# A decoder step on Trainium2: page rows made between GpSimd's stores, retention's first transposes one job later, the sample mix in five steps, and low halves of the output weights on GpSimd

## The chip, the cores and the metric

The kernel runs on one core of a Trainium2 chip. The metric is the device time of one execution in microseconds (us).

## The reference, cut to what matters

One step of a hybrid decoder layer is computed for 1024 prompt tokens and for 64 sample tokens (8 sequences of 8) with the same weights, in float32.

```python
def mixer_inputs(x, ln_g, w_in):
    h = rmsnorm(x, ln_g) @ w_in                 # 1024 x 3608, split into q, k, v, gates, z of three groups
...
def nsa_prompt(q, kv_c, kv_s, kv_w, gates, comp):      # 8 query heads, 2 key heads of 64
    o = gate0 * compressed + gate1 * selected_blocks + gate2 * window     # per block of 128 queries
def nsa_sample(...):
    past_c = pool_cmp[page_table]               # (8, 1024 tokens) gathered by page
    ...
    o = gates[:, :, 0] * o_c + gates[:, :, 1] * o_s + gates[:, :, 2] * o_w
def retention_chunk(state, q, k, v, log_g):     # 4 heads, recurrent over chunks
    ...
def mem_attend(q, mkv):                         # 4 heads over 256 memory tokens
def finish(x, o_n, z_n, o_r, z_r, o_m, z_m, w_out):
    mix = concat([o_n * silu(z_n), o_r * silu(z_r), o_m * silu(z_m)])
    return x + mix @ w_out                      # w_out 1024 x 1024, then a last rmsnorm
```

## The kernel before, in words

The kernel is one program with one instruction list for each engine, tied together by semaphores. It has two stages, which follow each other on every engine: the trunk and the attention.

**Splits.** Matrix products keep float32 precision by splitting each operand into a high half, rounded to TensorE's fast 32-bit type, and a low half, the operand minus its high half. A product is then three matmuls: high by high, low by high, high by low (`mm3`, L601 to L603; `mm3_turned`, L588 to L590, for results that come out transposed).

**The trunk** (`trunk`, from L414). The input projection is cut into jobs, one for each tile of 128 rows and chunk of 256 columns of the weights, 24 matmuls each. A job's sum lies in one of four PSUM banks. VectorE (for some chunks ScalarE) scales it into one of four staging buffers `a_hst` (L1125, L1127), and GpSimd stores that buffer in `h_scratch` (L744) and so makes it free again. ScalarE and VectorE split the weights of coming chunks (L564 and L577). Between the jobs stand groups of other work, from the list `groups` at L466: the compression of keys, then the retention. The latter is, for each of nine tiles, `r_t` (transposes on TensorE, L1189, of rows that GpSimd has multiplied with the rotary factors), `r_s` (scores), `r_o` (output and state updates). After it come `r_fin`, the load of the keys for the attention (`load_k`, L677 on SP's queue) and their transposes (`ktr`, L927). Each inner list is what stands behind one job. An empty group is a job with nothing behind it; four of them stand between `load_k` and the first `ktr`.

**Page rows.** The sample part gathers compressed keys through the page table. `pool_trunk` makes the row numbers first: it copies the page table into a scratch in memory, each entry repeated (L707), waits, reads it back with the entries on partitions (L709), waits, and makes row numbers in four small operations (L712 to L715). Then its loop over `b_steps` begins, in which the stores of the projection are. The gather itself is issued later in that loop.

**The attention** (`schedule`, from L1421). The queries are handled unit by unit, a unit being one block of queries and one head of one part. TensorE makes the scores (L1722, L1723), VectorE the maxima (L2047), ScalarE the exponentials (L1975), TensorE transposes them (L1745), ScalarE and VectorE copy the transposes out of PSUM (L1913), TensorE multiplies them with the values (L1866). VectorE weights the parts (`weights`, L2058) and normalizes (L2069), GpSimd adds the three branches and multiplies by z (`pool_mix_group`, L2223 to L2231), and stores the mixed rows.

The sample work goes in between, one group of the list `sample_groups` (L1403) for each unit. Its end is: `load_fin` brings the sample results back with tokens on partitions, `fin` mixes them, and then come the output weights in four quarters:

```python
        groups += [[("load_fin", 0)], [], [("fin", 0)], [], [], [], []]
        for m in range(4):
            groups += [[("w_hi", 2 * m)], [("w_lo", 2 * m)], [("w_hi", 2 * m + 1)], [("w_lo", 2 * m + 1)] + ([("load_w", m + 2)] if m < 2 else [])]
```

`w_hi` is a copy on ScalarE (L2016) of 1024 elements a partition, `w_lo` a subtraction on VectorE (L2176). Quarter m lies in buffer `d_wraw[m % 2]`, and SP loads it there (L1667). The first two quarters are loaded early. The load of quarter 2 overwrites the buffer of quarter 0, so it waits until low halves 0 and 1 are made, and that of quarter 3 until 2 and 3 are:

```python
                if n >= 2:
                    sp.wait_ge(S("dw_split"), 2 * (n - 1))
```

`fin` on GpSimd is one product of the three branches with their gates (L2320, 64 x 1536), then `pool_mix_sample` (L2210 to L2214: two products of 256, two sums and a product of 512), then the store into `mix_scratch` (L2323). Low half 4 overwrites memory that this store reads (`s_mxo`). Each engine works its list in order. The output projection (L1881 to L1887, `project`) follows on TensorE; it waits for all eight low halves.

## Time and profile before

| | |
|---|---|
| time, median of 3 runs | 939.58 us (938.59 to 940.44) |
| the profiled execution's own time | 939.63 us |
| its span | 937.8 us |
| TensorE busy | 95% of the span |
| VectorE busy | 56% |
| ScalarE busy | 44% |
| GpSimd busy | 31% |
| TensorE's clock granted | full in all 40 slices of the span |

The profile is of one execution. In it PE is TensorE's matmuls and PEld its weight loads, DVE is VectorE, ACT ScalarE, POOL GpSimd, and SPq the queue of SyncE (SP), from which most loads are issued. A row names the line of the kernel, the operation, what it writes and reads, and how often. Matmuls overlap, so their durations add up to more than the time that passes. In a timeline the bracket at the end of a row is the time that the engine stood idle before it and what released it.

### The profile page before, as it was taken

How to read it: one execution, taken by the hardware profiler on the slowest of the kernel's cores; microseconds unless marked ns; L12 is line 12 of the kernel's file. 1: busy time of each engine (PE TensorE's matmuls, PEld its weight loads, DVE VectorE, ACT ScalarE, POOL GpSimd, SP SyncE). 2: the span in 40 equal slices, each digit the busy share in tenths (PEclk: the TensorE clock that was granted, in tenths of full speed). 3: DMA queues.
4: the chain of work that ended last, by engine and by line, in shares of the span. 5: the costliest groups of instructions: out<-in, count | busy, mean ns of one | idle time of the engine just before them, and what ended most of it. 6: DMA issues, size and time to landing. Idle time of an engine off the chain costs nothing.

```text
span 937.8 us, 20464 instructions
## 1 busy us (share of the span) xinstructions
PE 895.2 (95%) x7594; PEld 811.5 (87%) x7594; DVE 524.2 (56%) x1501; ACT 413.7 (44%) x1063; POOL 291.0 (31%) x495
## 2 busy tenths in 40 slices
PE   6899999999999999999999999899999999999997
PEld 6899999999999899999988787768877787778885
DVE  4557332322323665645666787676777858844443
ACT  6434221224443011113466676565775667832221
POOL 0223212222223635435135153324422526410000
PEclk9999999999999999999999999999999999999999
DMA  7564414324240443231849058714604142343331
GB/s 230 156 206 136 151 45 152 103 88 121 67 145 25 132 142 98 95 105 63 219 132 284 4 160 264 255 57 119 181 2 131 56 141 77 102 137 133 128 121 67
DMA packets 85220, 117.91 MB, mean 126 GB/s; under 512 B 12930, under 2 KB 67506, under 8 KB 84546
## 3 DMA queue, kind: packets, MB, share of 16 engines
q1 hardware_dynamic: 71666, 73.12, 27.4%
q0 software_dynamic: 10224, 36.20, 11.5%
q10 hardware_dynamic: 3232, 7.28, 2.2%
q8 instruction: 61, 1.00, 0.5%
q14 instruction: 37, 0.30, 0.1%
HBM read 91.50 MB, written 32.02 MB: 132 GB/s over the span
## 4 chain that ended last, share of the span: by engine, by line
PE 78%; DVE 6%; issue 6%; ACT 5%; DMA 2%; POOL 2%; ACTq 0%; DVEq 0%; SPq 0%; POOLq 0%
PE psum L601 8%; PE psum L1866 7%; PE psum L602 7%; PE psum L603 7%; PE psum L1745 6%; PE psum L1722 4%; PE psum L1887 3%; PE psum L1886 3%; PE psum L1885 3%; PE psum L1723 3%; ACT p_P L1975 2%; PE psum L842 2%; PE psum L844 2%; PE psum L843 2%; PE psum L825 2%
## 5 line engine op out<-in xcount | busy, mean ns | idle before, releaser
L601 PE MATMUL psum<-a_whi,f_xhi 128*128 128x256 f32 (+1 forms) x672 | 194.7, 290 | 4.2 <-DVE a_hst L1127 2.6
L602 PE MATMUL psum<-a_wlo,f_xhi 128*128 128x256 f32 (+1 forms) x672 | 190.0, 283 | 0.0
L603 PE MATMUL psum<-a_whi,f_xlo 128*128 128x256 f32 (+1 forms) x672 | 189.6, 282 | 0.0
L1975 ACT ACTIVATE p_P<-psum,p_nb 128x640 f32<-128x640 f32 (+7 forms) x224 | 124.2, 561 | 45.8 <-DVE p_nb L2047 37.7
L601 PEld LDWEIGHTS psum<-a_whi,f_xhi 128*128 128x128 f32 x672 | 127.1, 189 | 6.9 <-DVE a_hst L1127 2.8
L602 PEld LDWEIGHTS psum<-a_wlo,f_xhi 128*128 128x128 f32 x672 | 127.2, 189 | 0.0
L603 PEld LDWEIGHTS psum<-a_whi,f_xlo 128*128 128x128 f32 x672 | 127.2, 189 | 0.0
L744 POOL DMA_DIRECT2D h_scratch<-a_hst x93 | 50.8, 548 | 211.7 <-DVE a_hst L1127 103.1
L1745 PE MATMUL psum<-f_ident,p_P 128*128 128x128 f32 x656 | 99.3, 275 | 1.4 <-ACT s_KTw L1925 0.7
L1745 PEld LDWEIGHTS psum<-f_ident,p_P 128*128 128x128 f32 x656 | 76.8, 140 | 8.0 <-DVE p_PT L1913 2.1
L2047 DVE CUSTOM_DVE_ANT_0 psum<-psum,p_near 128x256 f32<-128x256 f32 (+7 forms) x96 | 64.6, 673 | 31.2 <-PE psum L1723 25.3
L577 DVE SCALAR_TENSOR_TENSOR a_wlo<-a_wraw,c_gcol,a_whi 128x256 fp32r<-128x256 f32 (+1 forms) x120 | 63.6, 591 | 26.9 <-ACT a_whi L564 26.8
L1136 DVE TENSOR_TENSOR c_ctlo<-psum,c_cthi 128x512 fp32r<-128x512 f32 (+1 forms) x40 | 25.5, 637 | 93.4 <-ACT c_cthi L1022 93.4
L1866 PE MATMUL psum<-p_PT,p_V 128*64 128x128 f32 x1056 | 71.8, 279 | 3.5 <-issue 3.0
L1913 ACT COPY p_PT<-psum 128x512 f32<-128x512 f32 (+3 forms) x107 | 56.3, 526 | 38.2 <-PE psum L1745 36.8
L1866 PEld LDWEIGHTS psum<-p_PT,p_V 128*64 128x64 f32 x1056 | 56.4, 136 | 14.3 <-issue 13.0
L1022 ACT CAST c_cthi<-psum 128x512 fp32r<-128x512 f32 (+1 forms) x40 | 21.7, 544 | 105.8 <-PE psum L825 105.8
L588 PE MATMUL psum<-f_xhi,a_whi 128*128 128x256 f32 x192 | 55.5, 289 | 2.0 <-DVE a_hst L1125 2.0
L2228 POOL TENSOR_TENSOR p_Oi<-p_Oi 128x128 f32<-128x128 f32 x32 | 16.7, 523 | 125.8 <-DVE p_Oi L2069 125.8
L1913 DVE COPY p_PT<-psum 128x512 f32<-128x512 f32 (+3 forms) x109 | 54.9, 504 | 0.4 <-PE psum L1745 0.4
L589 PE MATMUL psum<-f_xhi,a_wlo 128*128 128x256 f32 x192 | 54.0, 281 | 0.0
L590 PE MATMUL psum<-f_xlo,a_whi 128*128 128x256 f32 x192 | 54.0, 281 | 0.0
(340 smaller groups left out, 2168.0 us busy)
## 6 DMA issues: line engine op xcount, KB each, us to landing
a_wraw<-in_w_in SPq DMA_DIRECT2D x24, 512.0 KB, 4.4
h_scratch<-a_hst POOLq DMA_DIRECT2D x72, 128.0 KB, 3.4
s_SG<-in_cache_nsa_slc SPq DMA_DIRECT2D x64, 128.0 KB, 2.3
p_qd<-q_scratch SPq DMA_DIRECT2D x16, 384.0 KB, 7.5
a_xraw<-in_x_prompt SPq DMA_DIRECT2D x8, 512.0 KB, 7.0
s_MK<-in_cache_mem SPq DMA_DIRECT2D x8, 512.0 KB, 8.6
s_WG<-in_cache_nsa_win SPq DMA_DIRECT2D x8, 512.0 KB, 5.3
mix_scratch<-p_zt POOLq DMA_DIRECT2D x8, 512.0 KB, 3.5
```

The costliest lines, as they stand in the source:

```text
L577: ins = nc.vector.scalar_tensor_tensor(out=lo[:, k], in0=raw[:, k], scalar=split_gain(e, 4 * half + k), in1=hi[:, k].bitcast(F32), op0=ALU ...
L588: nc.tensor.matmul(out, wh, hi, start=first, stop=False)
L589: nc.tensor.matmul(out, wl, hi, start=False, stop=False)
L590: return nc.tensor.matmul(out, wh, lo, start=False, stop=last)
L601: nc.tensor.matmul(out, hi, wh, start=first, stop=False)
L602: nc.tensor.matmul(out, hi, wl, start=False, stop=False)
L603: return nc.tensor.matmul(out, lo, wh, start=False, stop=last)
L1745: l = nc.tensor.transpose(o[0:w, 128 * j:128 * j + 128], P[v % 2][:, at:at + w], ident[:])
L1866: i_mm = nc.tensor.matmul(psum[64 * j:64 * j + 64, at:at + 128], val, PTs[p_rank[pair[j]] % NPT][0:w, 128 * p:128 * p + 128], start=k == 0 ...
L1913: copy(PTs[r % NPT][0:w, 0:128 * n], bank(4 + c % 3)[0:w, 0:128 * n]).then_inc(sem, 1)
L1975: nc.scalar.activation(dst, s_view(s), ACT.Exp, bias=nb[:, g % NNB:g % NNB + 1], scale=1.0 if s[2] == 3 else -1.0, accum_out=ssum[:, par[i ...
L2047: nc.vector.tensor_tensor_reduce(out=s_view(s), in0=s_view(s), in1=mask_view(v, s), scale=-1.0, scalar=3.0e38, op0=ALU.add, op1=ALU.min, a ...
```

## The change

There are four parts. The page table's way back and the four small operations move from before GpSimd's first store into the loop over the stores: the second transfer (`rows_back`) stands before the middle one of the stores ahead of the gather, and the small operations (`rows_made`) before the last one. One empty group is put ahead of the first `r_t`, and one is taken away after `load_k`. The mix of the sample rows is done in five steps, in five groups, with one product for each branch in place of a common one. And `w_lo` goes from VectorE's list to GpSimd's.

```diff
--- before.py
+++ after.py
@@ -466,13 +466,13 @@
             fetch = [("gather", u + 1)] if u + 1 < NITEM else [("load_rc", 0)]
             groups += [[tr(0)], [tr(1), hid(0), tr(2), hid(1)] + sec, [tr(3), ("regroup", a + 1), hid(2), hid(3), ("gelu", a)], fetch, [tr(4)],
                        [tr(5), hid(4)], [tr(6), hid(5), ("sec", a)], [tr(7), hid(6)] + ([("regroup", a + 2)] if u + 1 < NITEM else []), [hid(7), ("gelu", a + 1)]]
-        groups += [[], [("sec", NIDX - 1)], [("rrow", 0), ("r_init", 0), ("rope", 0)], [("rope", 1)], [], [("r_t", 0)], [("r_s", 0)]]
+        groups += [[], [("sec", NIDX - 1)], [("rrow", 0), ("r_init", 0), ("rope", 0)], [("rope", 1)], [], [], [("r_t", 0)], [("r_s", 0)]]
         for n in range(NT):
             groups.append([("r_t", n + 1)] if n + 1 < NT else [("r_z", 0)])
             groups.append([("r_o", n)] + ([("load_r", n + 2), ("rope", n + 2)] if n + 2 < NT else [("r_bd_out", 0)] if n == QT - 1 else []))
             groups.append([("r_s", n + 1)] if n + 1 < NT else [("r_o2", 0)])
             groups.append([])
-        groups += [[("r_fin", 0), ("r_s_out", 0), ("load_k", 0)], [], [], [], [], [("ktr", 0), ("ktr", 1)], [("ktr", 2), ("ktr", 3)], [("ktr", 4), ("maskb", 0)], [("qtr", 0), ("qtr", 1)], [("qtr", 2)]]
+        groups += [[("r_fin", 0), ("r_s_out", 0), ("load_k", 0)], [], [], [], [("ktr", 0), ("ktr", 1)], [("ktr", 2), ("ktr", 3)], [("ktr", 4), ("maskb", 0)], [("qtr", 0), ("qtr", 1)], [("qtr", 2)]]
         fill = []
         for j in range(2, NCH):
             tiles = (NT, NT + 1) if j in MEM_CHUNKS else range(NT)
@@ -705,14 +705,20 @@
         pool.wait_ge(S("vc_zero"), 1)
         pool.wait_ge(S("x_tr"), 6)
         pool.dma_start(pD[:, :, 0:1], io["page_table"].rearrange("b (p o q) -> (b p) o q", o=1, q=1).to_broadcast([NDB * NPG, NPG, 1]), allow_slow_non_contiguous=True).then_inc(S("row_in"), 16)
-        pool.wait_ge(S("row_in"), 16)
-        pool.dma_start(rowi[0][:], pD[:, :, 0].rearrange("(u j) c -> (j c) u", u=NDB // 2), allow_slow_non_contiguous=True).then_inc(S("row_in"), 16)
-        pool.wait_ge(S("row_in"), 32)
-        pool.wait_ge(S("const_in"), 16)
-        ch.step(pool.tensor_copy(rowf[:], rowi[0][:]))
-        ch.step(pool.tensor_scalar(rowf[:], rowf[:], float(NPG), None, ALU.mult))
-        ch.step(pool.tensor_tensor(rowf[:], rowf[:], colc[:, 18:19].to_broadcast([128, NDB // 2]), ALU.add))
-        ch.step(pool.tensor_copy(rowi[1][:], rowf[:]))
+
+        def rows_back():
+            pool.wait_ge(S("row_in"), 16)
+            pool.dma_start(rowi[0][:], pD[:, :, 0].rearrange("(u j) c -> (j c) u", u=NDB // 2), allow_slow_non_contiguous=True).then_inc(S("row_in"), 16)
+
+        def rows_made():
+            pool.wait_ge(S("row_in"), 32)
+            pool.wait_ge(S("const_in"), 16)
+            ch.step(pool.tensor_copy(rowf[:], rowi[0][:]))
+            ch.step(pool.tensor_scalar(rowf[:], rowf[:], float(NPG), None, ALU.mult))
+            ch.step(pool.tensor_tensor(rowf[:], rowf[:], colc[:, 18:19].to_broadcast([128, NDB // 2]), ALU.add))
+            ch.step(pool.tensor_copy(rowi[1][:], rowf[:]))
+
+        stores_before = [n for what, n in b_steps[:b_steps.index(("gather", 0))] if what == "ev"]
         for what, n in b_steps:
             if what == "gather" and n < NDB // 2:
                 if n >= 1:
@@ -733,6 +739,10 @@
             elif what == "ev":
                 j, t = proj_jobs[n]
                 r, w = tile_rows(t), w_n[j]
+                if n == stores_before[len(stores_before) // 2]:
+                    rows_back()
+                if n == stores_before[-1]:
+                    rows_made()
                 wait_evac(pool, n)
                 c = CHUNKS[j][1]
                 if turned(j, t):
@@ -1413,7 +1423,7 @@
                        [("t", ("kt", p, 1))], [("t", ("kt", p, 3))], [("t", ("ss", p, 1))], [("ms", p)], [("es", p)], [("t", ("st", p, 2))],
                        [("t", ("st", p, 3))], [("t", ("st", p, 0))], [("t", ("st", p, 1))], [("t", ("sv", p))] + ([("load_pair", p + 1)] if p + 1 < NPAIR else [("load_w", 0), ("load_w", 1)]),
                        [("store_pair", p)]]
-        groups += [[("load_fin", 0)], [], [("fin", 0)], [], [], [], []]
+        groups += [[("load_fin", 0)], [], [("fin", 0)], [("fin", 1)], [("fin", 2)], [("fin", 3)], [("fin", 4)]]
         for m in range(4):
             groups += [[("w_hi", 2 * m)], [("w_lo", 2 * m)], [("w_hi", 2 * m + 1)], [("w_lo", 2 * m + 1)] + ([("load_w", m + 2)] if m < 2 else [])]
         return groups
@@ -2168,12 +2178,6 @@
             elif what == "ms":
                 wait_chunk_read(dve, place["ss", n, 1])
                 sample_top(6, PSl[:], 3 * n + 3, "s_nb")
-            elif what == "w_lo":
-                dve.wait_ge(S("dw_hi"), n + 1)
-                if n == 4:
-                    dve.wait_ge(S("s_mxo"), 16)
-                m, ks = n // 2, slice(2 * (n % 4), 2 * (n % 4) + 2)
-                nc.vector.tensor_tensor(dwlo[m // 2][:, ks], dwraw[m % 2][:, 2 * (n % 2):2 * (n % 2) + 2], dwhi[m // 2][:, ks].bitcast(F32), ALU.subtract).then_inc(S("dw_split"), 1)
             elif what == "y":
                 r = tile_rows(D_ORDER[n])
                 if n == 0:
@@ -2203,15 +2207,25 @@
                                                    op0=ALU.mult, op1=ALU.mult).then_inc(S("d_y"), 1)
                 dve.wait_ge(S("d_y"), 2 * n + 2)
 
-    def pool_mix_sample(pool, ch):
+    def pool_mix_sample(pool, ch, n):
 
         z = zs[:, 0:512].rearrange("p (h d) -> p h d", d=HD)
         zm = zs[:, 768:1024].rearrange("p (h d) -> p h d", d=HD)
-        ch.do(pool.tensor_tensor(zs[:, 512:768], OC[0:NS_TOK, QT], zs[:, 512:768], ALU.mult))
-        ch.do(pool.tensor_tensor(zm, om_s[:], zm, ALU.mult))
-        ch.step(pool.tensor_tensor(on_s[:, :, 0], on_s[:, :, 0], on_s[:, :, 1], ALU.add))
-        ch.step(pool.tensor_tensor(on_s[:, :, 0], on_s[:, :, 0], on_s[:, :, 2], ALU.add))
-        pool.tensor_tensor(z, on_s[:, :, 0], z, ALU.mult).then_inc(S("s_mix"), 1)
+        g = gs[:].rearrange("p (r h o) -> p h r o", r=3, o=1)
+        if n == 0:
+            pool.wait_ge(S("on_in"), 16 * 2 * NDB)
+            pool.wait_ge(S("s_z"), 64)
+        if n < 3:
+            ch.step(pool.tensor_tensor(on_s[:, :, n], on_s[:, :, n], g[:, :, n].to_broadcast([NS_TOK, 8, HD]), ALU.mult))
+            if n:
+                ch.step(pool.tensor_tensor(on_s[:, :, 0], on_s[:, :, 0], on_s[:, :, n], ALU.add))
+        elif n == 3:
+            pool.tensor_tensor(zs[:, 512:768], OC[0:NS_TOK, QT], zs[:, 512:768], ALU.mult).then_inc(S("s_mix"), 1)
+            pool.tensor_tensor(zm, om_s[:], zm, ALU.mult).then_inc(S("s_mix"), 1)
+        else:
+            pool.tensor_tensor(z, on_s[:, :, 0], z, ALU.mult).then_inc(S("s_mix"), 1)
+            pool.wait_ge(S("s_mix"), 3)
+            pool.dma_start(mD[T:T + NS_TOK, :], zs[:]).then_inc(S("s_mxo"), 16)
 
     def pool_mix_group(pool, ch, n):
 
@@ -2306,6 +2320,12 @@
                 if n == last_block[i]:
                     pool.wait_ge(S("p_mix"), n + 1)
                     pool.dma_start(mD[128 * i:128 * i + 128, :], zt[par[i]][:]).then_inc(S(f"p_mxo{par[i]}"), 16)
+            elif what == "w_lo":
+                pool.wait_ge(S("dw_hi"), n + 1)
+                if n == 4:
+                    pool.wait_ge(S("s_mxo"), 16)
+                m, ks = n // 2, slice(2 * (n % 4), 2 * (n % 4) + 2)
+                pool.tensor_tensor(dwlo[m // 2][:, ks], dwraw[m % 2][:, 2 * (n % 2):2 * (n % 2) + 2], dwhi[m // 2][:, ks].bitcast(F32), ALU.subtract).then_inc(S("dw_split"), 1)
             elif what == "load_z":
                 load_z(n)
             elif what == "gates":
@@ -2314,13 +2334,7 @@
                 pool.wait_ge(S("d_y"), 2 * n + 2)
                 pool.dma_start(y_out(n, None), y_both(n)).then_inc(S(f"y_out{n % 2}"), 16)
             elif what == "fin":
-                pool.wait_ge(S("on_in"), 16 * 2 * NDB)
-                pool.wait_ge(S("s_z"), 64)
-                g = gs[:].rearrange("p (r h o) -> p h r o", r=3, o=1).to_broadcast([NS_TOK, 8, 3, HD])
-                ch.step(pool.tensor_tensor(on_s[:], on_s[:], g, ALU.mult))
-                pool_mix_sample(pool, ch)
-                pool.wait_ge(S("s_mix"), 1)
-                pool.dma_start(mD[T:T + NS_TOK, :], zs[:]).then_inc(S("s_mxo"), 16)
+                pool_mix_sample(pool, ch, n)
 
 
     with nc.Block() as block:
```

GpSimd's list at the start of the trunk before, from its first operation to its second store. `a_hst_68` to `a_hst_71` are the four staging buffers, `page_scratch` the scratch in memory, `f_rowi_59` the entries read back, `f_rowi_60` the row numbers:

```order
L707 DMA page_scratch<-in_page_table 512x1x1
L709 DMA f_rowi_59<-page_scratch 128x4x1
L712 CAST f_rowf<-f_rowi_59 128x4
L713 ISA
L713 TENSOR_SCALAR f_rowf<-f_rowf 128x4
L714 TENSOR_TENSOR f_rowf<-f_rowf,f_colc 128x4
L715 CAST f_rowi_60<-f_rowf 128x4
L744 DMA h_scratch<-a_hst_68 128x256
L744 DMA h_scratch<-a_hst_69 128x256
```

and with the change, from the sixth store on (the first page transfer and five stores stand ahead):

```order
L754 DMA h_scratch<-a_hst_69 128x256
L711 DMA f_rowi_59<-page_scratch 128x4x1
L754 DMA h_scratch<-a_hst_70 128x256
L754 DMA h_scratch<-a_hst_71 128x256
L754 DMA h_scratch<-a_hst_68 128x256
L754 DMA h_scratch<-a_hst_69 128x256
L754 DMA h_scratch<-a_hst_70 128x256
L716 CAST f_rowf<-f_rowi_59 128x4
L717 ISA
L717 TENSOR_SCALAR f_rowf<-f_rowf 128x4
L718 TENSOR_TENSOR f_rowf<-f_rowf,f_colc 128x4
L719 CAST f_rowi_60<-f_rowf 128x4
```

Eleven stores now stand ahead of the four small operations, six of them ahead of the transfer on which those wait. The gather keeps its place behind the twelfth store.

GpSimd's list near the end of the attention before, from the product of the three branches with their gates on. `s_on_s` are the branches, `s_zs` the z rows and the result, `p_Oi` and `p_zt` the prompt's blocks:

```order
L2320 TENSOR_TENSOR s_on_s<-s_on_s,s_gs 64x1536
L2210 TENSOR_TENSOR s_zs<-f_OC,s_zs 64x256
L2211 TENSOR_TENSOR s_zs<-s_om_s,s_zs 64x256
L2212 TENSOR_TENSOR s_on_s<-s_on_s 64x8x64
L2213 TENSOR_TENSOR s_on_s<-s_on_s 64x8x64
L2214 TENSOR_TENSOR s_zs<-s_on_s,s_zs 64x512
L2323 DMA mix_scratch<-s_zs 64x1024
L2223 TENSOR_TENSOR p_zt_125<-f_OC,p_zt_125 128x256
L2228 TENSOR_TENSOR p_Oi_150<-p_Oi_150 128x128
L2229 TENSOR_TENSOR p_Oi_150<-p_Oi_150 128x128
L2231 TENSOR_TENSOR p_zt_125<-p_Oi_150,p_zt_125 128x2x64
L2228 TENSOR_TENSOR p_Oi_151<-p_Oi_151 128x128
```

and with the change, from the last product of 256 on (three products of 512 and two sums in turn, and a product of 256 stand ahead), where `d_wlo`, `d_whi` and `d_wraw` are low halves, high halves and the weights as loaded:

```order
L2224 TENSOR_TENSOR s_zs<-s_om_s,s_zs 64x256
L2237 TENSOR_TENSOR p_zt_125<-f_OC,p_zt_125 128x256
L2242 TENSOR_TENSOR p_Oi_150<-p_Oi_150 128x128
L2243 TENSOR_TENSOR p_Oi_150<-p_Oi_150 128x128
L2245 TENSOR_TENSOR p_zt_125<-p_Oi_150,p_zt_125 128x2x64
L2226 TENSOR_TENSOR s_zs<-s_on_s,s_zs 64x512
L2228 DMA mix_scratch<-s_zs 64x1024
L2328 TENSOR_TENSOR d_wlo_194<-d_wraw_190,d_whi_192 128x1024
L2242 TENSOR_TENSOR p_Oi_151<-p_Oi_151 128x128
L2243 TENSOR_TENSOR p_Oi_151<-p_Oi_151 128x128
L2245 TENSOR_TENSOR p_zt_125<-p_Oi_151,p_zt_125 128x2x64
L2328 TENSOR_TENSOR d_wlo_194<-d_wraw_190,d_whi_192 128x1024
```

A prompt block now stands ahead of the last product of the sample mix, and another one between low halves 0 and 1. On VectorE's list the eight `d_wlo` rows are gone and the rest keeps its order.

## Rows read from the trace of the kernel before

**Rows 1.** The page, part 1: busy us (share of the span) xinstructions

```profile
PE 895.2 (95%) x7594; PEld 811.5 (87%) x7594; DVE 524.2 (56%) x1501; ACT 413.7 (44%) x1063; POOL 291.0 (31%) x495
```

**Rows 2.** Timelines of TensorE and VectorE at 42 us

```profile
42.66 0.39 PE L601 MATMUL psum<-a_whi,f_xhi 128*128 128x256 f32 x1 [2.60 <-DVE a_hst L1127]
42.12 0.48 DVE L1127 TENSOR_SCALAR a_hst<-psum,f_small 128x256 f32<-128x256 f32 x1 [6.01 <-DMA h_scratch<-a_hst]
```

**Rows 3.** Timeline of GpSimd, 0 to 60 us

```profile
17.41 0.83 POOL L707 DMA_DIRECT2D page_scratch<-in_page_table  x1 [15.60 <-PE psum L882]
29.85 0.82 POOL L709 DMA_DIRECT2D f_rowi<-page_scratch  x1 [11.62 <-DMA page_scratch<-in_page_table]
38.00 0.18 POOL L712 CAST f_rowf<-f_rowi 128x4 f32<-128x4 int32 x1 [7.33 <-DMA f_rowi<-page_scratch]
...
39.38 2.23 POOL L744 DMA_DIRECT2D h_scratch<-a_hst  x4 [0.32 <-POOL f_rowi L715]
```

**Rows 4.** Timelines of TensorE and VectorE, 299 to 309 us

```profile
305.41 0.60 PE L1189 MATMUL psum<-f_ident,r_ro 128*128 128x128 f32 x4
307.84 0.38 PE L588 MATMUL psum<-f_xhi,a_whi 128*128 128x256 f32 x1 [1.83 <-DVE a_hst L1125]
299.18 8.27 DVE L577 SCALAR_TENSOR_TENSOR a_wlo<-a_wraw,c_gcol,a_whi 128x256 fp32r<-128x256 f32 x4
```

**Rows 5.** Busy us: PE, PEld, DVE, ACT, POOL; PEclk, DMA share, GB/s

```profile
800.00:820.00 20.00, 18.54 (x183) 15.79 (x182) 17.35 (x49) 17.82 (x48) 6.30 (x10) 1.00 0.38 120
```

**Rows 6.** Timelines of SP, TensorE and VectorE; tile pk_Ktok

```profile
453.61 1.00 SPq L677 DMA_DIRECT2D pk_Ktok<-h_scratch  x2
460.93 1.03 PE L927 MATMUL psum<-f_ident,pk_Ktok 128*128 128x128 f32 x8
444.90 1.67 DVE L577 SCALAR_TENSOR_TENSOR a_wlo<-a_wraw,c_gcol,a_whi 128x256 fp32r<-128x256 f32 x4
DMA to landing us min/median/max: 3.9/4.5/5.2
```

**Rows 7.** Timeline of GpSimd, 782 to 797 us

```profile
782.67 2.81 POOL L2320 TENSOR_TENSOR s_on_s<-s_on_s,s_gs 64x1536 f32<-64x1536 f32 x1 [7.82 <-DMA s_om_s<-om_scratch]
785.55 1.66 POOL L2210 TENSOR_TENSOR s_zs<-f_OC,s_zs 64x256 f32<-64x256 f32 x1
787.18 0.73 POOL L2211 TENSOR_TENSOR s_zs<-s_om_s,s_zs 64x256 f32<-64x256 f32 x1
...
793.01 0.56 POOL L2323 DMA_DIRECT2D mix_scratch<-s_zs  x1 [0.29 <-POOL s_zs L2214]
...
796.85 0.46 POOL L2228 TENSOR_TENSOR p_Oi<-p_Oi 128x128 f32<-128x128 f32 x1
```

**Rows 8.** Groups by form of GpSimd: busy us, mean ns, idle us

```profile
L2285 POOL TENSOR_TENSOR p_QB<-p_qd,p_QA 128x512 fp32r<-128x512 f32 x21 | 26.9, 1280 | 1.7
```

**Rows 9.** Timeline of SP; the tile d_wraw, 785 to 795 us

```profile
791.61 8.68 SPq L1667 DMA_DIRECT2D d_wraw<-in_w_out  x2
DMA to landing us min/median/max: 5.1/5.1/5.1
```

**Rows 10.** Timelines of ScalarE and TensorE; the tile d_whi (ns)

```profile
801.31 1.04 ACT L2016 CAST d_whi<-d_wraw 128x1024 fp32r<-128x1024 f32 x1
804.33 0.36 PE L1722 MATMUL psum<-p_KM,p_QA 128*128 128x256 f32 x1 [1.02 <-ACT p_P L1975]
L2016 ACT CAST d_whi<-d_wraw x8: 1032/1038/1048, 784.0 to 813.5; 128x1024 fp32r<-128x1024 f32 x8
```

**Rows 11.** Timeline of VectorE; its groups, 780 to 822 us; line L2058 (ns)

```profile
785.42 1.21 DVE L2176 TENSOR_TENSOR d_wlo<-d_wraw,d_whi 128x1024 fp32r<-128x1024 f32 x1
L2176 DVE TENSOR_TENSOR d_wlo<-d_wraw,d_whi 128x1024 fp32r<-128x1024 f32 x8 | 10.4, 1302 | 1.9 <-ACT d_whi L2016 1.8
L2058 DVE SCALAR_TENSOR_TENSOR p_rw<-p_rw,p_gw x40: 161/168/1236, 496.7 to 827.3; 128x6 f32<-128x6 f32 x32, 128x4 f32<-128x4 f32 x8
```

**Rows 12.** The tile p_P on ScalarE, 780 to 822 us: waits, times

```profile
  DVE p_nb L2047: 2.0, 5
```

## The prediction

> **What bounds the kernel now.** I read the page's busy times first, then busy time by stretch, then each engine's timeline where the change works. TensorE is busy 95% of the span [rows 1]; what counts is only what makes it stand, or stand longer. Its busy time is partly modelled, so I look for gaps and for the chain of work behind them.
>
> There are three places. At 40 us TensorE stands for 2.60 us. Its release is a VectorE eviction (L1127), which had itself been idle 6.01 us for a staging buffer still waiting to be stored [rows 2]. The reason is on GpSimd [rows 3]: it issues the page-table transfer at 17.41, waits 11.62 us for it, issues the second one at 29.85, waits 7.33 us again, and only at 39.38 issues the first four stores. VectorE wanted the buffer at 42.12 - 6.01 = 36.1. At 307.84 TensorE stands for 1.83 us for an eviction of VectorE, which spent 8.27 us, from 299.18 on, on four splits of weights [rows 4]. From 800 to 820 us TensorE is busy 18.5 of 20 us, VectorE 17.4, ScalarE 17.8 [rows 5]: there all three feed each other, and a microsecond added to ScalarE or VectorE is a microsecond of TensorE. After that the output projection runs at TensorE's pace, and what is lost before it is not made good.
>
> **Part 1, page rows between the stores.** GpSimd now issues each of the first six stores as soon as its eviction is there. The second page transfer stands before the 7th store, the four small operations and their wait before the 12th. The 7th store comes no earlier than VectorE's 5th eviction at 36.1, and the first transfer had landed by 29.85, so its wait is over; the second took some 8 us (29.85 to 38.00) and is wanted about two pairs of evictions later. The gather is issued after the 12th store as before. Queued behind the two waits are stores alone, each with four buffers of slack. The gap goes: **-2.6 us**. Bounds: 0 if the stores land late (rival D), and 2.6, the whole gap. The four small operations (0.2 us each, 1.1 with the steps between them) lie in GpSimd's idle time.
>
> **Part 2, retention one job later.** TensorE's first four transposes (0.60 us at 305.41) lie today in the wait that ends at 307.84. That end comes from VectorE, behind its four splits, which are not moved. So the wait still ends there, and the transposes come after it: up to +0.6. Against it, the later pieces collide less with weight splits. I take **+0.3**, bounds -0.6 and +0.6. At the tail the key load comes a job later in SP's list, and its keys are transposed in the same place. It is issued at 453.61, what it takes is 5.2 us at most, and the transposes start at 460.93 [rows 6]. That leaves 460.93 - 453.61 - 5.2 = 2.1 us. VectorE's last four state updates start a job later, some 3 us, but the split of weights that stood between them (1.67 us [rows 6]) now stands ahead of them. So the load is issued some 1.4 us later and costs nothing. If that cover were gone it would cost what it is late.
>
> **Parts 3 and 4, sample mix in five steps and the low halves on GpSimd.** They must be costed together, since GpSimd works in order. It starts the mix at 782.67 for want of its data and cannot start sooner [rows 7]. The first row there has 1536 elements a partition and takes 2.81. The prices of GpSimd's two-input operations are 0.46 for 128 elements, 0.73 for 256 [rows 7] and 1.28 for 512 [rows 8], the last one's result of the rounded type: 0.27 for each 128 and 0.19 fixed. So a low half of 1024 elements takes 1.28 + 4 x 0.27 = 2.36, against 1.21 on VectorE [rows 11]. No row has one, and I take this line; bounds 2.2 and 3.3 (2.36 plus the 0.93 by which L2210 exceeded L2211).
>
> The time of GpSimd after the change, in the clock of the profile before: three products of 512 (2.81 and two more fixed shares, 3.2), two sums (2.5), two products of 256 (1.5), steps (0.3): 790.2. The mixing of a prompt block (one of 256 and three of 128, with steps 2.2): 792.4. Last product, wait, issue of the store (1.3 + 0.3 + 0.56): 794.5. Low half 0: 796.9. A prompt block of three operations (1.5): 798.4. Low half 1: **800.8**.
>
> That moment is what matters. SP's third weight load overwrites the buffer of low halves 0 and 1 and waits for both. Today the load is issued at 791.61, when VectorE has done them [rows 9]; now it is issued at 800.8, 9.2 us later. It takes 5.1 us [rows 9]: 805.9. But ScalarE reaches its fifth high-half copy, the first of that load, at 801.31 [rows 10]. So ScalarE, in order, stands for 4.6 us, and behind it wait the copy of transposed probabilities and the exponentials for which TensorE already waits today (1.02 us, until 804.33) [rows 10]. TensorE restarts at 808.9: **+4.6 us**. Bounds: 0 if something covers it (rival B), and 6.6 for low halves of 3.3. The fourth load: low halves 2 and 3 with a block between end at 807.1, it lands by 812.6. ScalarE's copies are (813.5 - 784.0) / 7 = 4.2 us apart [rows 10], the seventh at 809.3 today and at some 813.5 then, so about 1 us is left. The last low half is finished by 824, the projection needs it at 825.4 + 4.6.
>
> VectorE loses eight operations, 10.4 us with 1.9 of waits before them [rows 11]. What that gives is seen in ScalarE's waits for VectorE's maxima, 2.0 us in five [rows 12]. Before 801 it only lengthens the new wait. After 804 lies 18 of the 41 us of that stretch: **-0.9 us**, bounds 0 and -2.0.
>
> Here the two engines get in each other's way. L2210 took 1.66 where the equal L2211 took 0.73, and VectorE's low half started 0.13 before it [rows 7, 11]. VectorE's small weighting (L2058), whose inputs are both in SBUF, takes 0.168 as a rule and up to 1.236 [rows 11]. The Trainium skill (GPSIMD Engine Reference, section Key points) speaks against this change: GpSimd shares its SBUF interfaces with VectorE and contends with instructions that have two SBUF inputs; the trace agrees. By that rule at its hardest, five of L2058 in the stretch wait for a whole low half each, 11.8 us against the 10.4 saved, the relief is nothing, and the sum becomes +2.3. By the rows, VectorE's maxima and copies, with an input in PSUM, keep their times beside a busy GpSimd, and only an occasional L2058 waits: I keep -0.9.
>
> **Sum.** -2.6 + 0.3 + 4.6 - 0.9 = +1.4 on the profiled execution's 939.63 (span 937.8): **941.0**. The median of the runs is 939.58, 0.05 away. About 0.2%, 1.9 us, is what a measurement of this kernel can tell from no change, so 941.0 is no change, near the upper edge at 941.5. The case's own range is 939.2 to 942.5.
>
> **Rivals.**
> - **B, the load is in time.** ScalarE does not wait: 939.63 - 2.6 + 0.3 - 0.9 = 936.4. It needs 4.6 us from somewhere: faster strided products, a start of the mix before 782.67, or slack of TensorE behind ScalarE. For it: the prices of rows 7 come from a few operations, some lengthened by VectorE's low halves, which are gone. Against: GpSimd has no idle time in the chain, its start is set by a transfer, and TensorE waits for ScalarE in exactly this place.
> - **C, the low halves cost more, slower.** The mechanism is the sharing between GpSimd and VectorE, the place low halves 0 to 3. Each microsecond more per low half puts the third load 2 us later and the fourth 4. At 3.2 us each the first wait grows by 1.7 and the fourth load lands at 816.0 against a ScalarE that arrives at 815.2, 0.7 more: 943.4. It decides from 2.6 us a low half on. For it: the lengthened rows 7. Against: VectorE has few two-input operations left there.
> - **D, part 1 does not deliver.** The stores now share GpSimd's queue with page transfers in flight. Pieces of 4 bytes made these last 12 and 8 us; if the first stores land behind them later than 36.1, the gap stays: 943.6. By the Trainium skill (DMA: Bandwidth & Descriptors, section Two DMAs through the same engine are not ordered) descriptors of one queue start in order, so the stores would wait behind the first page transfer. The rows leave time for even that: it had landed at 29.85, and 6.3 us are left to 36.1, where four issued at once were back in 2.7.
>
> **How the numbers follow.** The forecast case 0.60 (no change 0.40, slower 0.15, faster 0.05, by its range), B 0.20, C 0.15, D 0.05. Faster by over 0.2%: 0.05 + 0.20 = 0.25. Within 0.2%: 0.40 + 0.02 of C = 0.42. Slower: 0.15 + 0.13 + 0.05 = 0.33. The range holds the forecast case, B with the relief at its bound (935.3), and C to 943.4: 935.3 to 943.4.
>
> **What would show it.** In the changed kernel: stores on GpSimd from about 26 us, no gap of TensorE at 40; a gap still at 305 to 308, then four transposes; the third output-weight load issued near 798.5 (all 2.3 us earlier than in my clock); a new wait of ScalarE of 4 to 5 us on that load before its fifth high-half copy, with a gap of TensorE of 5 us behind it; low halves of 2.4 us on GpSimd; fewer waits of ScalarE for maxima after it. I am wrong if the third load is issued before 794, if ScalarE's copy does not wait, or if low halves take over 2.6 us.

## The result, and the profile after

| | before | changed |
|---|---|---|
| median | 939.58 us (937.52 to 940.44, 5 runs) | 945.41 us (944.05 to 947.15, 5 runs) |
| ratio | 1 | 1.0066, 95% interval 1.0042 to 1.009 |
| profiled execution | 939.63, span 937.8 | 944.60, span 942.6 |

The change makes the kernel 5.8 us slower by the medians and 6.2 by the ratio. The forecast was 941.0, in a range up to 943.4. The page of the changed kernel, its busy times, and the slices for TensorE and its clock, to be held against [rows 1] and against the clock of before, which was full in all 40 slices:

```profile
PE 898.1 (95%) x7594; PEld 814.8 (86%) x7594; DVE 516.2 (55%) x1493; ACT 414.0 (44%) x1063; POOL 305.4 (32%) x505
...
PE   6999999999999999999999999989998999799997
...
PEclk9999999999999999999999999999999999899999
```

In slice 35 (801 to 825 us) TensorE is busy for 7 tenths, and there its clock is granted at 8 tenths. Busy as a share of the span it is 95% as before, so the share hides this; the busy time is 2.9 us longer (898.1 against 895.2) for the same 7594 matmuls. GpSimd's timeline there has the mix in five steps and the low halves (columns as before: start us, us, instruction, what released it):

```profile
780.94 2.15 POOL L2219 TENSOR_TENSOR s_on_s<-s_on_s,s_gs 64x512 f32<-64x512 f32 x2 [7.69 <-DMA s_om_s<-om_scratch]
...
790.58 1.27 POOL L2226 TENSOR_TENSOR s_zs<-s_on_s,s_zs 64x512 f32<-64x512 f32 x1
792.15 0.56 POOL L2228 DMA_DIRECT2D mix_scratch<-s_zs  x1 [0.29 <-POOL s_zs L2226]
792.72 2.38 POOL L2328 TENSOR_TENSOR d_wlo<-d_wraw,d_whi 128x1024 fp32r<-128x1024 f32 x1
795.05 0.46 POOL L2242 TENSOR_TENSOR p_Oi<-p_Oi 128x128 f32<-128x128 f32 x1
...
796.55 4.69 POOL L2328 TENSOR_TENSOR d_wlo<-d_wraw,d_whi 128x1024 fp32r<-128x1024 f32 x2
```

As forecast, the mix begins when its data are there (780.94, against 782.67 in [rows 7]), and a low half takes 2.38 us (the forecast took 2.36 by a line through shorter operations). Low half 1 is done at 798.9. The load that waits for it, the wait of ScalarE for the load and that of TensorE for ScalarE, in the timelines of SP, ScalarE and TensorE (they answer to [rows 9, 10]):

```profile
798.94 6.49 SPq L1677 DMA_DIRECT2D d_wraw<-in_w_out  x2
803.83 1.04 ACT L2026 CAST d_whi<-d_wraw 128x1024 fp32r<-128x1024 f32 x1 [5.06 <-DMA d_wraw<-in_w_out]
800.35 0.60 PE L1755 MATMUL psum<-f_ident,p_P 128*128 128x128 f32 x4
806.86 0.55 PE L1732 MATMUL psum<-p_KM,p_QA 128*128 128x256 f32 x1 [5.91 <-ACT p_P L1985]
```

The load is issued at 798.94, the forecast said 798.5. ScalarE stands 5.06 us (forecast 4.6), TensorE 5.91 us where it stood 1.02 before. Busy time by stretch, columns as in [rows 5], shows what was not forecast:

```profile
800.00:805.00 5.00, 0.95 (x8) 0.71 (x7) 2.65 (x6) 1.18 (x2) 4.84 (x6) 1.00 0.60 210
805.00:810.00 5.00, 3.14 (x16) 2.84 (x18) 1.25 (x4) 4.67 (x15) 2.32 (x2) 0.58 0.81 260
810.00:815.00 5.00, 5.00 (x45) 4.50 (x43) 2.31 (x8) 2.19 (x8) 3.69 (x4) 0.74 0.70 212
815.00:820.00 5.00, 5.00 (x50) 4.10 (x46) 3.17 (x11) 4.82 (x10) 2.38 (x1) 1.00 0.00 0
```

and in steps of 2 us:

```profile
806.00:808.00 2.00, 1.14 (x5) 1.18 (x6) 0.00 (x0) 2.00 (x9) 1.32 (x1) 0.50 0.95 239
808.00:810.00 2.00, 2.00 (x13) 1.67 (x13) 1.25 (x4) 1.67 (x5) 0.00 (x0) 0.50 1.07 411
810.00:812.00 2.00, 2.00 (x18) 1.67 (x15) 0.35 (x1) 0.45 (x2) 1.41 (x4) 0.50 1.04 313
812.00:814.00 2.00, 2.00 (x16) 2.00 (x16) 0.99 (x4) 0.74 (x2) 2.00 (x1) 0.84 0.72 217
814.00:816.00 2.00, 2.00 (x27) 1.66 (x26) 1.07 (x4) 2.00 (x6) 0.51 (x2) 1.00 0.00 0
```

When TensorE starts again at 806.86 its clock is granted at 0.50, which is 1.2 of 2.4 GHz. Worked out from the stretches, it had fallen at some 805.8, while TensorE stood, and it stays at half until some 812.6. Before, the clock was full there. The Trainium skill (TensorE: Matmul & The Clock Gate, section What's actually happening) says that an engine which has been idle falls back to 1.2 GHz and gets 2.4 only after it has been busy again. The trace agrees with that: 5.91 us of idleness, then half the clock.

At the other end of the program GpSimd's stores come early, and the gap at 40 us is gone (rows answering to [rows 3]; no wait of TensorE for `a_hst` over 0.2 us is left there):

```profile
17.59 0.83 POOL L707 DMA_DIRECT2D page_scratch<-in_page_table  x1 [15.78 <-PE psum L892]
26.90 1.11 POOL L754 DMA_DIRECT2D h_scratch<-a_hst  x2 [8.48 <-DVE a_hst L1137]
...
36.97 1.07 POOL L754 DMA_DIRECT2D h_scratch<-a_hst  x2 [5.48 <-DVE a_hst L1137]
38.03 0.78 POOL L711 DMA_DIRECT2D f_rowi<-page_scratch  x1
...
56.39 0.19 POOL L716 CAST f_rowf<-f_rowi 128x4 f32<-128x4 int32 x1
```

### The profile page after: what moved, and what is told of

It reads as the page before. It is cut to its first block, busy times and chain, and to the rows that moved or that the text cites. A ratio compares the mean times of both kernels' runs of the same rounds, so it can differ in the third digit from the quotient of the medians.

```text
span 942.6 us, 20464 instructions
## 1 busy us (share of the span) xinstructions
PE 898.1 (95%) x7594; PEld 814.8 (86%) x7594; DVE 516.2 (55%) x1493; ACT 414.0 (44%) x1063; POOL 305.4 (32%) x505
## 4 chain that ended last, share of the span: by engine, by line
PE 79%; DVE 6%; issue 4%; POOL 4%; DMA 3%; ACT 3%; SPq 1%; ACTq 0%; DVEq 0%; POOLq 0%
PE psum L601 9%; PE psum L602 8%; PE psum L603 8%; PE psum L1876 7%; PE psum L1755 5%; PE psum L1732 3%; PE psum L1897 3%; PE psum L1896 3%; PE psum L1895 3%; PE psum L1733 2%; PE psum L852 2%; PE psum L854 2%; PE psum L853 2%; PE psum L835 2%; PE psum L588 2%
## 5 line engine op out<-in xcount | busy, mean ns | idle before, releaser
L2242 POOL TENSOR_TENSOR p_Oi<-p_Oi 128x128 f32<-128x128 f32 x32 | 14.6, 455 | 120.2 <-DVE p_Oi L2079 120.2
```

## The experiments

### How the kernels are compared

Single executions differ by 2 us and more in the trunk and in the middle of the attention, whatever the kernel. So two measures are used. One is the ratio of the timed runs with its interval, 0.11 to 0.25% to either side. The other is a stretch of the profile that hardly varies: from TensorE's transposes of the 32nd block of results (`p_OT`, 772.16 before, 770.56 changed) over its restart behind ScalarE's fifth high half (804.33 and 806.86) to the first matmul of the output projection (825.38 and 830.18). Each entry is a difference of starts in TensorE's timeline; the clock is that of the stretch from 800 to 820 us.

| kernel | ratio (95%) | median us | to the restart | restart to projection | both | clock |
|---|---|---|---|---|---|---|
| before | 1 | 939.45 to 940.2 | 32.17 | 21.05 | 53.22 | 1.00 |
| changed | 1.0066 (1.0042 to 1.009) | 945.41 | 36.30 | 23.32 | 59.62 | 0.83 |
| e12_after, the same again | 1.0072 (1.0054 to 1.009) | 945.73 | 36.30 | 23.20 | 59.50 | 0.83 |
| e1_rows, part 1 alone | 1.0000 (0.9987 to 1.0013) | 940.01 | 32.34 | 21.06 | 53.40 | 1.00 |
| e2_ret, part 2 alone | 0.9995 (0.9981 to 1.0009) | 939.45 | 32.25 | 21.03 | 53.28 | 1.00 |
| e3_mix, part 3 alone | 0.9994 (0.998 to 1.0007) | 939.97 | 31.79 | 21.06 | 52.85 | 1.00 |
| e4_low, part 4 alone | 1.0064 (1.0049 to 1.008) | 945.49 | 36.08 | 23.47 | 59.55 | 0.83 |
| e6_no4, parts 1 to 3 | 0.9993 (0.998 to 1.0006) | 938.73 | 32.76 | 21.04 | 53.80 | 1.00 |
| e9_late, before, load 3 late | 1.0068 (1.0043 to 1.0093) | 945.70 | 37.56 | 23.07 | 60.63 | 0.83 |
| e5_fill, changed, gap filled | 1.0035 (1.0021 to 1.0049) | 943.64 | 36.48 | 20.67 | 57.15 | 1.00 |
| e7_first, quarter 0 first | 0.9971 (0.9956 to 0.9985) | 937.35 | 30.90 | 20.67 | 51.57 | 1.00 |
| e8_half, halves 4 to 7 on GpSimd | 0.9986 (0.9971 to 1.0000) | 938.30 | 33.20 | 20.66 | 53.86 | 1.00 |
| e10_base, e7 without 1 and 2 | 0.9986 (0.9971 to 1.0002) | 938.10 | 30.92 | 20.67 | 51.59 | 1.00 |
| e11_noret, e7 without 2 | 0.9971 (0.996 to 0.9982) | 936.28 | 30.92 | 20.67 | 51.59 | 1.00 |

The ratios are to the kernel before, run on the same chip in each set; its medians there were 940.2, 939.5 and 939.45.

### Each part alone

The four parts of the change, each put alone into the kernel before. The edits are the hunks of the diff above; these are lines or parts of lines from them, in order for e1_rows, e2_ret (which also takes an empty group away behind `load_k`), e3_mix and e4_low (which keeps the mix in one piece, ahead of the low halves):

```diff
+                if n == stores_before[len(stores_before) // 2]:
+                    rows_back()
...
-[("rope", 1)], [], [("r_t", 0)], [("r_s", 0)]]
+[("rope", 1)], [], [], [("r_t", 0)], [("r_s", 0)]]
...
-        groups += [[("load_fin", 0)], [], [("fin", 0)], [], [], [], []]
+        groups += [[("load_fin", 0)], [], [("fin", 0)], [("fin", 1)], [("fin", 2)], [("fin", 3)], [("fin", 4)]]
...
-                nc.vector.tensor_tensor(dwlo[m // 2][:, ks], dwraw[m % 2][:, 2 * (n % 2):2 * (n % 2) + 2], dwhi[m // 2][:, ks].bitcast(F32), ALU.subtract).then_inc(S("dw_split"), 1)
+                pool.tensor_tensor(dwlo[m // 2][:, ks], dwraw[m % 2][:, 2 * (n % 2):2 * (n % 2) + 2], dwhi[m // 2][:, ks].bitcast(F32), ALU.subtract).then_inc(S("dw_split"), 1)
```

e1_rows. 

> The kernel before with part 1 alone (page rows between the stores). My theory: the gap of TensorE at 40 us goes, 2.6 us less: 937.0, ratio 0.997. Rival (the stores in the page transfer's queue land late, or the time is given back later in the attention): 939.6, ratio 1.000.

e2_ret. 

> The kernel before with part 2 alone (retention one job later). My theory: the wait of TensorE near 307 stays and the four transposes come behind it, +0.3 to +0.7: 940.1, ratio 1.0005. Rival (the shifted splits collide less and win): 938.5 or less.

e3_mix. 

> The kernel before with part 3 alone (sample mix in five steps, low halves still on VectorE). My theory: nothing on the path waits for the mix, 939.6, ratio 1.000, and the third load of output weights stays near 791.6. Rival (GpSimd's products slow VectorE's low halves and the mix ends late): 1 us more, 940.6.

e4_low. 

> The kernel before with part 4 alone (low halves on GpSimd, mix in one piece). My theory: the third load waits for GpSimd, which makes low half 0 behind the mix; ScalarE stands some 4 us for it, TensorE 5 us, and TensorE's clock is granted at half for some 8 us behind the gap: +7 to +8, 947. Rival (the damage comes from the five steps and GpSimd's sharing with VectorE, not from the load): +1 to +3, and no wait of ScalarE over 1 us.

Part 4 alone makes the whole loss: 1.0064 against 1.0066, and 59.55 against 59.62 us in the stretch. The 947 expected was 1.5 too high. Its timelines show the same chain, with the mix in one piece ahead:

```profile
L2308 POOL TENSOR_TENSOR d_wlo<-d_wraw,d_whi x8: 2341/2376/2380, 791.9 to 821.1; 128x1024 fp32r<-128x1024 f32 x8
...
  DMA d_wraw<-in_w_out: 4.9, 1
```

The tile of the loaded weights: low halves from 791.9 on, and 4.9 us in which ScalarE sat idle until the load landed. Part 3 alone gains 0.4 us in the stretch and nothing that the timed runs can tell. Part 2 alone neither gains nor loses.

Part 1 alone was the surprise. It should have given 2.6 us, and its interval excludes more than 1.2. Two things take the gain away. First, the 2.60 us of [rows 2] were the worst of the executions seen. In the other five profiles of kernels with the old page rows TensorE stood at 40 us for 0.6 (e2_ret), 1.1 (e3_mix), 0 (e4_low), 0 (e9_late) and 1.0 us (e10_base), on average 0.9 with the kernel before. One thing that varies is the second page transfer, the idle time ahead of the cast, as these rows of GpSimd of e4_low and e3_mix show against 7.33 us in [rows 3]:

```profile
33.31 0.18 POOL L712 CAST f_rowf<-f_rowi 128x4 f32<-128x4 int32 x1 [3.79 <-DMA f_rowi<-page_scratch]
```

```profile
35.01 0.18 POOL L712 CAST f_rowf<-f_rowi 128x4 f32<-128x4 int32 x1 [4.28 <-DMA f_rowi<-page_scratch]
```

Another is how long the first stores take to land. In e2_ret they were issued at 35.72, 3.7 us earlier than before, but VectorE got its buffer at 40.61, only 1.5 us earlier: 4.9 us after the issue, where it had been 2.7.

Second, part 1 brings a new wait. At the start of the attention GpSimd loads the gates; its idle time ahead of that load is 1.47 us in every profile without part 1 (six) and 2.47 us in every profile with it (eight), and in the latter no semaphore explains it ("issue"). Later in the same list it makes the low halves of a query block, and TensorE waits for these. GpSimd's row of before and of e1_rows, and TensorE's waits from 490 to 500 us in e1_rows (us in total, times, longest):

```profile
486.06 0.54 POOL L2254 DMA_DIRECT2D p_gt<-h_scratch  x1 [1.47 <-DMA out_new_mem<-a_hst]
```

```profile
485.32 0.54 POOL L2264 DMA_DIRECT2D p_gt<-h_scratch  x1 [2.47 <-issue]
```

```profile
PE psum L1732 <- POOL p_QB L2295: 0.8, 1, 0.8
```

Before there is no such wait. In all eight kernels with part 1 it is 0.55 to 0.84 us; of the six without it only e9_late has one, of 0.25. So 0.9 us on average are gained at 40 us, and some 0.7 are given back at 498. That these two make up the whole of the missing gain is worked out from single profiles and not tested by itself. Why the list needs 1 us more there is open; it was not tried.

### Is it GpSimd, or the late load?

e9_late leaves all work where it was before and makes only the third load late:

```diff
                 if n >= 2:
-                    sp.wait_ge(S("dw_split"), 2 * (n - 1))
+                    sp.wait_ge(S("dw_split"), 4)
```

> The kernel before, nothing on GpSimd changed; only the third load waits for low halves 0 to 3 instead of 0 and 1, so it is issued near 799.8 and lands near 804.9, 3.6 us after ScalarE wants it at 801.3. Theory (lateness of the load alone makes the loss): ScalarE waits 3.6, TensorE stands some 4.5 to 5, its clock falls behind that, +5 to +6: 945.5. Rival (a GpSimd cause): 940 to 942.

```profile
798.50 0.95 SPq L1667 DMA_DIRECT2D d_wraw<-in_w_out  x2
805.31 1.04 ACT L2016 CAST d_whi<-d_wraw 128x1024 fp32r<-128x1024 f32 x1 [5.29 <-DMA d_wraw<-in_w_out]
808.34 0.55 PE L1722 MATMUL psum<-p_KM,p_QA 128*128 128x256 f32 x1 [6.42 <-ACT p_P L1975]
```

```profile
805.00:810.00 5.00, 1.66 (x8) 1.69 (x9) 3.05 (x8) 4.33 (x12) 0.00 (x0) 0.59 0.97 302
810.00:815.00 5.00, 5.00 (x39) 4.46 (x37) 3.40 (x8) 2.81 (x8) 2.28 (x3) 0.72 0.02 8
```

The first three are timeline rows of SP, ScalarE and TensorE, the other two busy time by stretch (PEclk is the third number from the end). The load is issued at 798.50, ScalarE stands 5.29 and TensorE 6.42 us, the clock reads 0.59 and 0.72 in the two stretches around and behind the restart, and the time is 945.7, the changed kernel's. GpSimd had no part in it. ScalarE's wait is 1.7 us longer than the 3.6 expected: the third load, issued 0.4 us ahead of the fourth, took 6.8 us to land and not 5.1.

e6_no4, the changed kernel with the low halves back on VectorE:

> The changed kernel with the low halves back on VectorE (parts 1 to 3 alone). Theory (the whole loss is the late third load): 939.5, ratio 0.9995, third load issued before 792. Rival (the five steps or the moved retention carry part of it): 941 or more.

```profile
788.80 9.07 SPq L1677 DMA_DIRECT2D d_wraw<-in_w_out  x2
```

The third load is issued at 788.80 (SP's timeline), the time is 938.73 and the stretch 53.80 us: with the load in time the loss is gone.

### Is half of it the clock?

e5_fill lets TensorE work while it would stand. Behind the transposes of the unit just ahead of the wait it makes them twelve times more, the same values to the same place:

```diff
                 for j, (a, k, w) in enumerate(tiles):
                     ...
+                if v == 133:
+                    for _ in range(12):
+                        for j, (a, k, w) in enumerate(tiles):
+                            at = sms[a][7] + 128 * k
+                            l = nc.tensor.transpose(o[0:w, 128 * j:128 * j + 128], P[v % 2][:, at:at + w], ident[:])
```

> The changed kernel; TensorE repeats the four transposes that it makes just before its long wait twelve times more (same values to the same place, some 5.6 us), so that it works through most of the 5.9 us in which it stood. The late load and ScalarE's wait of 5 us stay. Theory (half the loss behind the late load is the clock, which is granted at half after the gap): the clock stays full in 800 to 820, and the time is 2.3 to 3.3 less than the changed kernel's 945.4: 942.6. Rival (the wait alone costs, TensorE behind it is bound by the other engines): 945.4, whatever the clock.

```profile
802.85 5.40 PE L1760 MATMUL psum<-f_ident,p_P 128*128 128x128 f32 x48
809.13 0.36 PE L1732 MATMUL psum<-p_KM,p_QA 128*128 128x256 f32 x1 [0.87 <-ACT p_P L1990]
806.09 1.05 ACT L2031 CAST d_whi<-d_wraw 128x1024 fp32r<-128x1024 f32 x1 [5.26 <-DMA d_wraw<-in_w_out]
```

```profile
805.00:810.00 5.00, 4.13 (x37) 3.92 (x36) 0.81 (x2) 3.91 (x12) 4.43 (x2) 1.00 0.44 116
810.00:815.00 5.00, 5.00 (x60) 4.47 (x58) 3.64 (x11) 4.40 (x12) 3.45 (x4) 1.00 1.05 350
```

Again timeline rows, of TensorE and ScalarE, and two stretches. ScalarE waits for the load as long as before (5.26 us), TensorE restarts as late (36.48 us into the stretch, against 36.30), but it has stood for 0.87 us only, and its clock is full. From the restart to the projection it takes 20.67 us where the changed kernel takes 23.32: **2.65 us are the clock's**. The timed runs agree in direction: 1.0035 against 1.0072 for the changed kernel run again, with intervals that don't touch, and against 1.0066 for its first runs, whose interval overlaps by a little (1.0042 against 1.0049). The size is less sure there than in the stretch: the time, 943.64, is 1.0 above the 942.6 expected and 1.8 to 2.1 below the changed kernel's medians, while the ratios are 2.9 to 3.5 us apart. The other numbers of this column say the same: 21.05 in the five kernels with all low halves on VectorE and a full clock, 20.67 in the five with at least the last four on GpSimd and a full clock, 23.1 to 23.5 in the four where the clock fell (so some 2.0 us for it in e9_late, whose low halves are on VectorE).

### Repairs

e7_first keeps the whole change and turns the order in the list round: the first quarter's two high and two low halves and the third load come ahead of the mix.

```diff
-        groups += [[("load_fin", 0)], [], [("fin", 0)], [("fin", 1)], [("fin", 2)], [("fin", 3)], [("fin", 4)]]
+        groups += [[("load_fin", 0)], []]
         for m in range(4):
             groups += [[("w_hi", 2 * m)], [("w_lo", 2 * m)], [("w_hi", 2 * m + 1)], [("w_lo", 2 * m + 1)] + ([("load_w", m + 2)] if m < 2 else [])]
+            if m == 0:
+                groups += [[("fin", 0)], [("fin", 1)], [("fin", 2)], [("fin", 3)], [("fin", 4)]]
```

> The changed kernel, but the first quarter's four steps (high halves 0 and 1 on ScalarE, low halves 0 and 1 on GpSimd, third load) stand ahead of the five steps of the mix instead of behind them. Theory (the order in GpSimd's list makes the load late, not GpSimd's slower low halves): the third load is issued before 785, no wait of ScalarE for it, clock full in 800 to 820, 939.0, ratio 0.999. Rival (low halves of 2.4 us on GpSimd hurt by sharing with VectorE): 941 to 943.

```profile
782.75 0.40 SPq L1679 DMA_DIRECT2D d_wraw<-in_w_out  x1
775.56 2.37 POOL L2330 TENSOR_TENSOR d_wlo<-d_wraw,d_whi 128x1024 fp32r<-128x1024 f32 x1
780.35 2.37 POOL L2330 TENSOR_TENSOR d_wlo<-d_wraw,d_whi 128x1024 fp32r<-128x1024 f32 x1 [2.42 <-ACT d_whi L2028]
784.86 2.15 POOL L2221 TENSOR_TENSOR s_on_s<-s_on_s,s_gs 64x512 f32<-64x512 f32 x2
...
795.90 2.39 POOL L2330 TENSOR_TENSOR d_wlo<-d_wraw,d_whi 128x1024 fp32r<-128x1024 f32 x1
803.80 0.36 PE L1734 MATMUL psum<-p_KM,p_QA 128*128 128x256 f32 x1 [0.74 <-ACT p_P L1987]
```

Rows of SP, GpSimd and TensorE. GpSimd makes low halves 0 and 1 in the time in which it had waited for the data of the mix; the third load is issued at 782.75, TensorE's wait at this place is 0.74 us, and a low half still costs 2.37 to 2.39. The stretch takes 51.57 us, 1.65 less than before, and the time is 937.35, better than the 939.0 expected: the interval of the ratio ends at 0.9985, it is faster than both kernels. The rival, that the low halves do harm on GpSimd as such, falls.

e8_half leaves only low halves 4 to 7 on GpSimd, counted on a semaphore of their own:

```diff
-            elif what == "w_lo":
+            elif what == "w_lo" and n >= 4:
...
+            elif what == "w_lo" and n < 4:
```

The first is GpSimd's step, the second VectorE's.

> The changed kernel with low halves 0 to 3 back on VectorE and 4 to 7 left on GpSimd. Theory (only the halves on which loads wait do harm): both loads in time, clock full, VectorE relieved of four operations: from block 31 to the projection 52.5 us, the time 938.0, ratio 0.998. Rival (GpSimd's sharing with VectorE costs by itself): no better than parts 1 to 3 alone, 938.7 or more.

938.30 with an interval up to 1.0000: both loads are in time, but of the forecast gain in the stretch (52.5) nothing is there. Behind the restart it has the same 20.66 as the repair, ahead of it 33.20, more than before (32.17). Rows of VectorE and GpSimd show a part of the reason:

```profile
784.92 2.35 DVE L2185 TENSOR_TENSOR d_wlo<-d_wraw,d_whi 128x1024 fp32r<-128x1024 f32 x1
784.91 1.28 POOL L2226 TENSOR_TENSOR s_on_s<-s_on_s 64x512 f32<-64x512 f32 x1
```

Low half 0 on VectorE starts 0.01 us behind one of GpSimd's sums and takes 2.35 us in place of 1.21 [rows 11]. The four low halves on VectorE take 7.1 us together where the same four took 5.5 before, 6.0 in e6_no4 (32.76 ahead of the restart) and 5.7 in e3_mix (31.79). So where the low halves stay on VectorE, the mix in steps can make them longer; why e3_mix needs less than before all the same is open. It is open too how much of the repair's gain ahead of the restart is VectorE's relief and how much the turned order: that order with all low halves on VectorE was not run.

e10_base, the repair in the kernel before, without parts 1 and 2:

> The kernel before with part 3, part 4 and the first quarter ahead of the mix, without parts 1 and 2. Theory (the gain of the repaired version is all near the end, 1.6 us from block 31 to the projection; part 1 gives about 1 us in the trunk and gives 0.7 back at the start of the attention): 937.7, ratio 0.998. Rival (part 1 brings the gain): 939.5.

e11_noret, the repair without part 2:

> The repaired version (first quarter ahead of the mix) without the retention shift. Theory (part 2 is worth nothing either way): 937.3, the same as the repaired version. Rival (part 2 costs its 0.3 to 0.7): 936.8.

Both have 51.59 us in the stretch. So the repair's gain is there and does not need parts 1 and 2, though in the timed runs alone e10_base is not clear of the kernel before (0.9971 to 1.0002). **e11_noret** is the best version by its median, 936.28 (0.9971, interval 0.996 to 0.9982), but it and e7_first can't be told apart, so whether part 2 costs anything stays undecided, and e10_base, at 938.10, overlaps both; what part 1 adds on top stays open within 2 us.

e12_after, the changed kernel again:

> The changed kernel itself again, on the chip of the runs around it, for its spread: 945.4, the clock under 0.9 in 800 to 820 in its profile, block 31 to the projection 59.6 us.

It came out as expected, to 0.1 us in the stretch.

## Why the prediction was wrong

The forecast was 1.4 us more, measured are 5.8. The step that failed is the one behind the wait: the sum ended with TensorE's restart and put the slower clock behind it at nothing; it cost 2.65 us. The difference of 4.4 us is two terms: 2.7 in the stretch (6.4 against 4.6 - 0.9), which is the clock, and 1.7 for parts 1 and 2, which were to give 2.3 (2.6 less 0.3) and gave 0.6 by the medians (5.8 against 6.4), 0.2 by the ratio, and nothing that e1_rows and e2_ret could measure. In the two profiled executions the account closes: block 31 starts 1.60 us earlier, the stretch is 6.40 longer, behind it both need 112.4 us, and the spans differ by 4.8.

- **The late load: right, in place, cause and size.** Third load issued at 798.94 (forecast 798.5), ScalarE's wait 5.06 (4.6), TensorE's restart 4.13 us later than before, counted from block 31 (4.6). For the fourth load the recorded working has a slip: 807.1 and 5.1 are 812.2 and not 812.6. It changes nothing in the sum; the load was in time.
- **What lies behind that wait: wrong.** The step "TensorE restarts at 808.9: +4.6 us" ended there, as if everything behind went on at its old pace. The range's upper bound for the wait (6.6) held longer low halves and nothing of the clock, and no rival had it. The runs show 2.65 us for it. By the parts as measured the stretch is 4.13 - 0.38 + 2.65 = 6.40 us longer. The forecast's 4.6 - 0.9 = 3.7 comes close to 4.13 - 0.38 = 3.75 partly by luck: both terms were some 0.5 too large and cancel. The clock was in the traces from the start as a row that read full in all slices; the question that was not asked is what a gap of 5 to 6 us does to it.
- **VectorE's relief of 0.9: too large here.** The term counted what lies behind the wait, and that is 0.38 (21.05 against 20.67 at a full clock). Ahead of it, as the prediction said, time saved only lengthens the wait: TensorE came to it 0.76 us sooner, stood 4.89 longer (5.91 - 1.02), and restarted 4.13 later, when the load let it. With the load in time it counts: e7_first gains 1.65 us in the stretch over before, 1.27 of it ahead of the restart, within the bound of 2.0.
- **Part 1, "the gap goes: -2.6 us": wrong size.** The gap goes in every profile with part 1. But its length was read from one execution, in which the second page transfer took some 8 us; the mean of six is 0.9, and some 0.7 come back as a wait near 498 us. By e1_rows it is worth 0, and no more than 1.2. The lower bound of the term was 0 and right, for a reason (rival D, late stores) that did not occur.
- **Part 2, +0.3: too small to see.** In the changed kernel the wait near 307 us stays (2.26 us, against 1.83), and the transposes come behind it, as forecast; the keys' transposes at the tail start without a wait (457.88). e2_ret measures 0.9995 (0.9981 to 1.0009).
- **Rival B** (the load is in time) did not occur, but e7_first is what it described, and its time, forecast at 936.4, was 937.35. **Rival C** (low halves dearer by sharing) fell: on GpSimd they take 2.34 to 2.39 us in all profiles.
- **The sharing of GpSimd with VectorE** is real, and small in the changed kernel. There VectorE's small weighting takes up to 2.10 us beside a low half; these are its line (ns min/median/max), its group from 778 to 830 us and GpSimd's low halves (groups: busy us, mean ns):

```profile
L2068 DVE SCALAR_TENSOR_TENSOR p_rw<-p_rw,p_gw x40: 164/167/2101, 493.7 to 832.1; 128x6 f32<-128x6 f32 x32, 128x4 f32<-128x4 f32 x8
```

```profile
L2068 DVE SCALAR_TENSOR_TENSOR p_rw<-p_rw,p_gw 128x6 f32<-128x6 f32 x5 | 3.1, 628 | 0.2
L2328 POOL TENSOR_TENSOR d_wlo<-d_wraw,d_whi 128x1024 fp32r<-128x1024 f32 x8 | 18.8, 2365 | 1.5 <-ACT d_whi L2026 1.5
```

and the group in the kernel before, 780 to 826 us:

```profile
L2058 DVE SCALAR_TENSOR_TENSOR p_rw<-p_rw,p_gw 128x6 f32<-128x6 f32 x5 | 2.1, 428 | 0.2
```

Five weightings take 3.1 us in place of 2.1, 1 us against the 10.4 of low halves that VectorE lost [rows 11]. In the kernel before, VectorE's own low halves had lengthened GpSimd's operations (1.66 us for L2210), and that is gone (0.73 for the same product). The hardest reading of the Trainium skill (GPSIMD Engine Reference, section Key points), that each of the five waits for a whole low half, would have made it 11.8. The trace shows it for one of the five, the one of 2.10 us: it starts at 799.16, 0.2 us into a low half, and ends with it at 801.2. Of the others one took 0.54 and three 0.17.

## What to carry to other kernels

When a change makes the bounding engine stand for several microseconds, price the clock behind the gap as well as the gap: here half the clock for some 6 us behind the restart added 2.65 to a gap that had grown by 4.9, and a kernel whose clock reads full everywhere has this to lose. When work moves to an idle engine, ask what stands ahead of it in that engine's list: the low halves on GpSimd lost 0.6% when the first two stood behind the mix, and with these ahead of it the kernel gained 0.1 to 0.3%, with the same durations. And don't price a wait that hangs on a small transfer from one execution; TensorE's wait for it went from 0 to 2.6 us between executions with the same page-row code.
